# A transformer kernel's mixing stage: products in another order on two PSUM banks, with norms, values, gating and the first head's start between them

## The reference

```python
hn = modulate(rms_norm(h, g_mix[l]), ...)             # 256 tokens and 256 context tokens
q_lat, kv_lat, k_pe, sg_in, cv_in = split(hn @ w_mix_in[l])   # 384, 256, 32, 512, 768 wide
q  = rope(rms_norm((rms_norm(q_lat) @ w_q_up) per head))      # 8 heads of 96
kv = (rms_norm(kv_lat) @ w_kv_up) per head                    # k: 64 of 96, v: 64
k  = rope(rms_norm(concat(k_nope, k_pe)))
attn = softmax(q k^T / sqrt(96)) v                            # keys: tokens and context
u, v = split(gelu(sg_in)); v = rms_norm(v in 4 groups)
sg = u * (w_spatial @ v + b_spatial)                          # per chunk of 128 tokens
y  = conv3(c_gate * xin);  cv = b_gate * y                    # cv_in = b_gate, c_gate, xin
h  = h + gate * concat(rms_norm(attn), rms_norm(sg), rms_norm(cv)) @ w_mix_out
```

## Time and profile before

| | us |
|---|---|
| median of 3 runs | 3660.41 |
| lowest, highest | 3659.3, 3660.67 |
| the profiled execution, its whole time | 3657.16 |
| its span on the core | 3655.5 |

### The profile page before, as it was taken

The page is one execution under the profiler, slowest core; times in us unless marked ns, Lnnn a source line. Parts: engine busy times, 40 slices in busy tenths (PEclk is TensorE's granted clock), DMA queues, the critical chain, the costliest instruction groups (busy, mean ns, idle before and its releaser), DMA issues.

```text
span 3655.5 us, 43446 instructions
## 1 busy us (share of the span) xinstructions
PE 3493.5 (96%) x16116; PEld 2591.0 (71%) x16116; DVE 1419.6 (39%) x3403; ACT 661.0 (18%) x1299; POOL 41.1 (1%) x80
## 2 busy tenths in 40 slices
PE   7999998989999999999899999999999999978999
PEld 4888855555888878887657885455478885555788
DVE  3444522333444554454242002456254554244100
ACT  2000022551000020001252002334210001233100
POOL 0000000000000000000000000000000000000000
PEclk8999999989999999999899999999999999988999
DMA  5443231543222232224274447464032224574443
GB/s 222 160 161 133 87 114 56 198 145 111 96 82 89 88 122 82 92 82 145 83 295 173 153 151 170 71 52 52 30 135 89 87 87 130 83 76 35 167 150 109
DMA packets 114634, 424.28 MB, mean 116 GB/s; under 512 B 12864, under 2 KB 16064, under 8 KB 112320
## 3 DMA queue, kind: packets, MB, share of 16 engines
q1 hardware_dynamic: 104256, 376.49, 29.5%
q0 software_dynamic: 7872, 42.73, 10.1%
q10 hardware_dynamic: 2368, 3.10, 0.2%
HBM read 412.83 MB, written 1.05 MB: 113 GB/s over the span
## 4 chain that ended last, share of the span: by engine, by line
PE 87%; DMA 5%; DVE 3%; ACT 2%; issue 2%; SPq 0%; POOL 0%; DVEq 0%; ACTq 0%
PE PS L756 27%; PE PS L808 16%; PE PS L689 11%; PE PS L870 7%; PE PS L1084 5%; DMA mix<-arena 3%; PE PS L1075 3%; PE PS L829 2%; PE PS L621 2%; DMA ring<-stream 2%; PE PS L906 2%; PE PS L1154 1%; PE PS L1136 1%; PE PS L672 1%; PE PS L990 1%
## 5 line engine op out<-in xcount | busy, mean ns | idle before, releaser
L689 PE MATMUL PS<-xn,ring 128*128 128x256 f32 (+1 forms) x1664 | 419.6, 414 | 4.9 <-issue 4.8
L689 PEld LDWEIGHTS PS<-xn,ring 128*128 128x128 f32 x1664 | 315.2, 190 | 109.0 <-issue 71.2
L756 PE MATMUL PS<-xn,ring 128*128 128x256 f32 x1312 | 302.4, 384 | 4.2 <-DMA ring<-stream 2.1
L756 PEld LDWEIGHTS PS<-xn,ring 128*128 128x128 f32 x1312 | 248.3, 191 | 58.5 <-issue 19.1
L1084 PE MATMUL PS<-xn,arena 128*128 128x512 f32 (+1 forms) x640 | 283.0, 564 | 6.6 <-ACT mix L1480 5.2
L870 PE MATMUL PS<-arena,ring 128*128 (+2 forms) x1120 | 271.6, 405 | 0.0
L870 PEld LDWEIGHTS PS<-arena,ring 128*128 128x128 f32 x1120 | 214.0, 191 | 56.4 <-issue 30.4
L808 PE MATMUL PS<-xn,ring 128*128 128x256 f32 x752 | 223.6, 379 | 0.0
L808 PE MATMUL PS<-arena,ring 128*128 128x256 f32 x784 | 202.1, 380 | 0.3
L808 PE MATMUL PS<-xn 128*128 128x256 f32 x752 | 193.0, 379 | 0.0
L1084 PEld LDWEIGHTS PS<-xn,arena 128*128 128x128 f32 x640 | 115.1, 201 | 98.4 <-issue 85.5
(11 more groups left out here) (261 smaller groups left out, 4536.2 us busy)
## 6 DMA issues: line engine op xcount, KB each, us to landing
ring<-stream SPq DMA_DIRECT2D x716, 512.0 KB, 3.4
arena<-pair_m POOLq DMA_DIRECT2D x8, 1536.0 KB, 7.1
arena<-pair_n POOLq DMA_DIRECT2D x8, 1024.0 KB, 5.1
arow<-arena POOLq DMA_DIRECT2D x24, 256.0 KB, 21.4
mix<-head_w POOLq DMA_DIRECT2D x16, 320.0 KB, 3.3
mix<-na_bias POOLq DMA_DIRECT2D x8, 512.0 KB, 16.2
mix<-masks POOLq DMA_DIRECT2D x1, 2048.0 KB, 8.8
mix<-arena POOLq DMA_DIRECT2D x8, 256.0 KB, 38.8
```

The source lines that it names most:

```text
L689: m = pe.matmul(PS[:, bank, 0:tokens], ring[:, s, k * P:(k + 1) * P], xn[:, k, 0:tokens], start=k == 0, stop=k == DC - 1)
L756: m = pe.matmul(out, weights, moving, start=k == 0, stop=k == 3)
```

## The change

All products of `mix_in` now use two banks in turn (`MIX_BANKS`), and so do the value tiles. The gating products come right behind the first six units, the u units behind these, and the convolution's units last, ordered by half (`CV_ORDER`). Between the products TensorE now makes the sums and spreads of q_lat and kv_lat, head 0's projection, the spatial products, head 0's rotation, sums and spreading, the norms of sg and cv, and the values. ScalarE and VectorE have matching orders, each written out in its `mix_in`. The phases of these norms, values and gating stay in the plan for their counts, but no engine runs them as phases (`made_beside`). The norms of sg and cv stand ahead of the heads, so that only attn's is left before `down`. Squares go to places of their own in `arena` (`squares`). The number of units, matmuls and bytes is unchanged.

```diff
-MERGED_BANKS = (1, 2, 3)
-VALUE_BANKS = (2, 3, 4, 7)
+ATTN_BANK = 1
+MIX_BANKS = (3, 2)
+GATING_BANKS = (4, 5)
+FM_BEFORE, FM_BESIDE = QC + KC + 1, 8
+CV_ORDER = ((1, 0), (2, 0), (0, 0), (1, 1), (2, 1), (0, 1))
...
         phase("gating", layer=l, tokens=tokens, tiles=tiles, adds=dict(sg=1))
+        norm("sg", 2, tokens, 1, False, l)
+        norm("cv", 2, tokens, 1, False, l)
...
         phase("turn", layer=l, tokens=tokens, tiles=tiles, adds=dict(merge=4))
         norm("attn", 4, tokens, 1, False, l)
-        norm("sg", 2, tokens, 1, False, l)
-        norm("cv", 2, tokens, 1, False, l)
```

TensorE's `mix_in`; `more()` makes the next of the eight units for u and the convolution:

```diff
-                for j in range(MIX_FM):
-                    pe.wait_ge(acc_evacuated, ph.at.evac + j - 3)
...
+                def bank_of(a):
+                    pe.wait_ge(acc_evacuated, ph.at.evac + a - 1)
+                    return MIX_BANKS[a % 2]
...
+                for j in range(FM_BEFORE):
+                    fm(j, ph.tokens if j < QC else TOK)
+                pe.wait_ge(ada_done, q.at.ada)
+                norm_sums(q)
+                norm_sums(kv)
+                for t in range(ph.tiles):
+                    gate_tile(t)
+                    if t == 1:
+                        norm_roots(q, 0)
+                        norm_roots(kv, 1)
+                more()
+                pe.wait_ge(norm_scaled, sgn.at.scaled)
+                project(hd, 0, 0)
+                project(hd, 0, 1)
+                more()
+                more()
+                gating(gat)
+                pe.wait_ge(head_raw, 2 * hd.at.head + 2)
+                rotate(1, kpe_rot)
+                more()
+                sums(0)
+                more()
+                spread_roots(0)
+                more()
+                norm_sums(sgn)
+                more()
+                norm_roots(sgn, 2)
+                more()
+                s = unit_in(ph.at.unit, U_MIX)
+                for t in range(4):
+                    if t < 2:
+                        pe.wait_ge(acc_evacuated, ph.at.evac + made[0] - 1 + t)
+                    else:
+                        pe.wait_ge(value_copied, val.at.values + t - 1)
+                    value_tile(s, t)
+                    if t == 1:
+                        norm_sums(cvn)
+                norm_roots(cvn, 0)
+                pe.wait_ge(value_copied, val.at.values + 4)
```

ScalarE's `mix_in`, its later part; `parts` are the copies of the convolution's units, `hval` holds the values:

```diff
+                copy(sgu[:, 1, :], ph.tokens, ACT.Gelu_apprx_tanh)
+                act.wait_ge(sg_var, gat.at.sg + 1)
...
+                parts[0]()
+                parts[1]()
+                roots(0)
+                parts[2]()
+                parts[3]()
+                act.wait_ge(sg_done, gat.at.sg + 1)
+                for c in range(2):
+                    square(sgn, c)
+                std_of(sgn)
+                parts[4]()
+                parts[5]()
+                for t in range(4):
+                    act.wait_ge(value_ready, val.at.values + t + 1)
+                    act.activation(hval[:, t, :], PS[:, MIX_BANKS[t % 2], :], ACT.Copy).then_inc(value_copied, 1)
+                    if t == 0:
+                        act.wait_ge(cv_done, gat.at.sg + 1)
+                        for c in range(2):
+                            square(cvn, c)
+                    if t == 1:
+                        std_of(cvn)
+                link(act.activation(root_table[:, :], eps[0:1, :], ACT.Exp))
```

VectorE's `mix_in` from the spatial products on; the dots stand for gating's product with u, which ends in `sg_done`:

```diff
+                dve.wait_ge(kpe_rot, l + 1)
+                rope(1, kpe_rotated)
...
+                roots(0)
+                convolution(0)
+                link(gated(0))
+                normed(0)
+                root(sgn, 2)
+                convolution(1)
+                scale(sgn)
+                gated(1).then_inc(cv_done, 1)
+                root(cvn, 0)
+                scale(cvn)
```

More of the change, by code:

```diff
@@ L463, in norm_spec, with beside, made_beside, squares @@
             return s
+        def beside(ph):
+            i = PLAN.index(ph)
+            return PLAN[i + 1:i + 8]
+        def made_beside(ph):
+            return ph.kind in ("values", "gating") or ph.kind == "norm" and ph.what in ("q_lat", "kv_lat", "sg", "cv")
+        def squares(ph):
+            at = {"q_lat": 25, "kv_lat": 28, "sg": 21, "cv": 23}.get(ph.what, 24)
+            return arena[:, at:at + ph.chunks, :]
         def norm_bank(ph):
@@ L649, in norm @@
                     pe.wait_ge(seven_folded, last_down(ph).at.fold + 3)
[L650 to L655, removed]
+                norm_sums(ph)
                 if ph.ada:
@@ L967, in spread_roots, with heads @@
                     m.then_inc(head_spread, 1)
+                return rotate, sums, spread_roots
+            def heads(ph):
+                tiles, H0, T0 = ph.tiles, ph.at.head, ph.at.headtile
+                rotate, sums, spread_roots = heads_before(ph)
                 def scores(i, t):
@@ new lines, in copy @@
+                def copy(to, tokens, how=ACT.Copy):
+                    act.activation(to[:, 0:tokens], bank_in()[:, 0:tokens], how).then_inc(acc_evacuated, 1)
+                for j in range(QC):
+                    copy(qlat[:, j, :], ph.tokens)
+                copied_all()
+                for c in range(QC):
+                    square(q, c)
+                for j in range(KC):
+                    copy(kvlat[:, j, :], TOK)
+                copied_all()
+                for c in range(KC):
+                    square(kv, c)
@@ new lines, in mix_in @@
+                link(act.activation(root_table[:, :], eps[0:1, :], ACT.Sqrt))
+                bank = bank_in()
+                act.activation(qkraw[64:128, 1, :], bank[64:128, :], ACT.Copy,
+                               scale=col("g_k_head", ph.layer)[64:128, :])
+                act.activation(qkt[64:128, 1, :], bank[64:128, :], ACT.Square).then_inc(acc_evacuated, 1)
+                std_of(q)
+                std_of(kv)
+                for t in range(ph.tiles):
+                    copy(sgv[:, t, :], SG, ACT.Gelu_apprx_tanh)
@@ L1403, in roots, with heads @@
                                        scale=1.0 / QK).then_inc(head_std, 1)
+                return raw, roots
+            def heads(ph):
+                tiles, T0 = ph.tiles, ph.at.headtile
+                raw, roots = heads_before(ph)
                 def exps(i, t):
@@ L1559, in _ @@
             run = dict(ada=ada, norm=norm, swiglu=swiglu, down=lambda ph: None, mix2=lambda ph: None, mix_in=mix_in, up7=up7, down7=down7,
-                       values=lambda ph: None, gating=gating, heads=heads, turn=turn, gates=gates, pairs=pairs, mlp=mlp)
+                       heads=heads, turn=turn, gates=gates, pairs=pairs, mlp=mlp)
             for ph in PLAN:
-                if ph.kind == "norm" and ph.what in ("q_lat", "kv_lat"):
-                    act.wait_ge(acc_evacuated, ph.at.evac)
-                run[ph.kind](ph)
+                if not made_beside(ph):
+                    run[ph.kind](ph)
         @block.vector
@@ L1919, in normed, with heads @@
                     ins.then_inc(head_rope, 1)
+                return rope, roots, normed
+            def heads(ph):
+                tiles, T0 = ph.tiles, ph.at.headtile
+                rope, roots, normed = heads_before(ph)
                 def maxes(i, t):
```

236 lines of the change are left out of this document (122 added, 114 removed).

## The result

The changed kernel takes **3623.0 us** (median of 4 runs, 3616.6 to 3623.8) against 3659.9 us for the kernel before (4 runs): a ratio of 0.990, with a 95% interval of 0.988 to 0.991. The forecast was 3627, with a range of 3619 to 3642. The profiled execution spans 3621.2 us, 34.3 less than that of before.

The account below looks back on a forecast made before the run. TensorE is busy 3493.5 of 3655.5 us, so only its idle or low-clock time can be won. Terms 9.7 + 2.1 + 12.0 + 2.3 + 3.2 + 3.6 = 32.9 us, from 3660.4 to 3627; range 3619 to 3642.

Parts of the forecast that it names:

- Prologue of layer 0: From mix_in's products to head 0's scores: idle time and low clock removed, less moved work and new waits, 9.7 us won.
- The wait before sg's sums: Layer 0's prologue: ScalarE squares sg behind a unit's copy, so TensorE waits 1.5 and 0.3 us for the two squares.
- The wait at the loop's branch: Start of the head loop: a wait on the last value copy, taken as 0.5 us, bounds 0 and 1.3.
- Prologue of layer 1: The same stretch in layer 1, with units of 256 columns and thinner cover: 12.0 us won.
- The draw at `vpad`: Layer 1, spatial products: `vpad` needed and ready both at 22.8 us; bounds 0 and 1 us of waiting, 0.3 taken.
- First iterations: Head 0's iteration starts at full clock: 2.1 us won in layer 0, 2.3 us in layer 1.
- Tail of layer 0: Only attn is spread before `down`, which starts 5.8 us sooner but loses 2.6 to low clock: 3.2 us won.
- Tail of layer 1: `down` starts 4.1 us sooner, with 0.5 more of low clock than today: 3.6 us won.
- the falling clock: Rival: the clock falls and returns at four cuts a layer, 17.6 us lost, giving 3645 us; chance 0.08.
- the missing overlap: Rival: with two banks each product waits for its predecessor's copy, 27 us go back, giving 3654 us; chance 0.04.
- The lasting fall: Rival: the clock stays low from the latents' sums to the scores in both layers, 147 us lost, 3774 us; chance 0.02.
- The better case: No new wait shows and `down` finds its clock at once: 3620 us; chance 0.04 for below 3619.

Follow-up runs that it names:

- tail_undone: The changed kernel with only the norms of sg and cv put back behind the heads, in a row with attn's: 3620.8 us.
- changed_again: The changed kernel run once more with no edit: 3624.4 us, ratio 0.991 to the kernel before.
- One bank: The changed kernel with all products of the stage and the value tiles in one bank, each waiting for the copy of the one before: 3645.0 us.
- early_squares: The changed kernel with ScalarE squaring sg ahead of the copy of the fourth convolution unit instead of behind it: 3616.7 us, ratio 0.989.
- warm_tail: The changed kernel with matmuls on constants in the last head's waits and around attn's sums and spreading: 3617.5 us, ratio 0.989.

## Why the prediction was right

- **Prologue of layer 0: 9.7 expected, 11.1 measured.** Idle time went from 10.4 to 1.3 us, and all narrow groups run at full clock. The wait before sg's sums was there (1.21 us of idle time and 0.3 between its two squares, visible as 0.94 us for sums that take 0.64). The wait at the loop's branch, taken at 0.5, was nothing: the copy is covered by cv's spread (627.63 to 628.66, with no idle time behind it), and tail_undone, without that spread, waits 0.89 there. These two terms give back 0.9 us; the other 0.5 is the two spreadings of 16 records, which take 1.78 us from start to next start (594.37 to 596.15) where 2.05 was taken.
- **Prologue of layer 1: 12.0 expected, 11.8 measured.** The draw at `vpad` went well, with no idle time before `L1008`. TensorE waited 0.78 us before sg's sums where 1.3 was taken, 0.22 before the scores where 0.4 was taken, and the branch cost nothing. Narrow work used this up. The added sums and spreads of sg and cv, a term of 1.5 us, measured 2.55 from start to next start (0.64, 0.64, 0.56 and 0.71). The sums of the latents take 1.22 us where I had 0.9, and a unit of 256 columns beside a narrow group takes 0.1 to 0.2 us more than its 3.45. That the total came within 0.2 us is luck: the terms missed by more than 1 us each way.
- **First iterations: 2.1 and 2.3 expected, 2.1 and 2.3 measured.** They ran at full clock from the start.
- **Tail of layer 0: 3.2 expected, 2.5 measured.** From attn's sums to `down` 6.7 us instead of 12.1, 5.4 sooner against 5.8 expected: a spread of 8 records by itself takes 2.08 us, not a third of the 5.39 for 24. `down` loses 2.9 us to the clock against 2.6, and 1.9 in changed_again.
- **Tail of layer 1: 3.6 expected, 3.9 measured,** 3.7 sooner (expected 4.1) and `down` 0.26 us shorter, not 0.5 longer. Here too two errors cancel. The loss varies: `down` takes 29.4 to 30.3 us in the three traces of the changed kernel, and the tail wins 3.0 to 5.2.
- **The sum:** 32.9 expected between the spans, 34.3 measured. The median was to be 3.25 us above the profiled execution, as before; it lies 0.1 above it. That offset is most of the 4 us between 3627 and 3623, and it is scatter, which the sum could not foresee. The upper end of the span of 3620 to 3637 does not follow from its bounds: with the waits doubled, 1.3 twice at the branch and 3.2 twice for `down`, it comes to 3634. The measured median lies inside either.
- **The rivals.** One bank refutes the falling clock, for waits up to 1.2 us, and the missing overlap at once. The lasting fall is refuted by the result's windows, at 1.00 over both stages. The better case did not come: early_squares and warm_tail show what its two conditions, no new wait and `down` at full clock, are worth, 2.5 and 7.8 us by stages. The Trainium skill ("TensorE: Matmul & The Clock Gate", "A second HAM failure mode: psum-queue depth-cycling") tells of a kernel whose clock swung as it idled briefly between groups while cycling through PSUM banks. That did not happen here: even one bank for all products, with 0.5 to 0.8 us of waiting between groups, leaves the clock at 1.00. That kernel's own case, bf16 products of 512 columns, was not tried.
- **What the prediction did not say** although its terms held it: the norms' move nets nothing (6.8 won in the tails against 4.6 of work and 3.2 of waits). The gain is that of the filled prologue, with the clock that came back in it and in the first iterations.

## What to carry to other kernels

Where a chain of short steps across three engines stands behind a block of independent products, put the products between its links. Nearly every link gave back its wait, and the clock came with it. Before moving a step out of one gap into a full stretch, charge it there at its full-clock price plus the wait of its operand, and look at whether the copy in an engine's fixed order stands ahead of what the next step waits for: one copy moved behind two squares was worth 2.5 us here. Where waits remain, a few matmuls on constants won 4 us a tail; they brought `down` to 2.4 GHz each time, though they did not keep the clock up all the way in each execution.

## What the runs showed of the hardware

- The granted clock stayed at 2.4 GHz (1.00) through layer 0's head loop and through one_bank's stages, with waits of 0.5 to 1.3 us between dense groups. In layer 0 of the changed kernel it fell at the end of the last head's iteration, with its narrow products of 64 columns and waits of 0.5 to 0.7 us (1.00 in 786 to 788 us, 0.52 in 788 to 790), and stayed at 1.2 GHz until `down` had run for some microseconds (0.57 in 806 to 809 us, 1.00 behind).
- The same program gets the clock back, or loses it, at other points from one execution to the next: in layer 1 of changed_again it fell only behind attn's sums (0.95 in 1904 to 1906 us, 0.50 in 1906 to 1908), layer 1's `down` takes 29.4 or 30.3 us, and the same 535 records take 179.3 or 186.9 us. With the profiled spans of one kernel between 3616 and 3634 us, edits worth 2 to 3 us are read from stages, not from medians.
